# Last norm of a three-layer block: the running sum of squares moves from VectorE to GpSimd

## The reference, cut to what matters

```python
def rms_norm(x, g):
    xf = x.astype(jnp.float32)
    xf = xf * lax.rsqrt(jnp.mean(xf * xf, axis=-1, keepdims=True) + RMS_EPS)
    return xf.astype(x.dtype) * g

        x = x + hierarchical_moe(h2, ...)     # the experts' results, added to the residual
    return rms_norm(x, final_norm_g)          # over the 1024 features of each token
```

## Time and profile before

| | us |
|---|---|
| median of 3 executions | 1638.87 |
| lowest and highest of them | 1638.64, 1643.22 |
| the profiled execution, its time | 1638.95 |
| its span, first to last instruction | 1637.1 |
| around the span | 1.85 |

### The profile page before, as it was taken

How to read it: one execution, slowest core, us unless ns; L and a number is a source line. 1 busy time by engine, 2 the same in 40 slices (tenths; PEclk the granted TensorE clock), 3 DMA queues, 4 the chain that set the end, 5 groups by cost and what they waited for, 6 DMA issues and landing times.

```text
span 1637.1 us, 20086 instructions
## 1 busy us (share of the span) xinstructions
PE 1595.3 (97%) x7426; PEld 1203.3 (73%) x7426; DVE 845.6 (52%) x1456; ACT 583.0 (36%) x963; POOL 547.6 (33%) x239
## 2 busy tenths in 40 slices
PE   7999999999999999999999999999999999999997
PEld 5888768887888888887877667888877885444543
DVE  5447577125655546344668686343242644343434
ACT  4127454334332225324533342343243333112213
POOL 4441226731444444751334123455424410000000
PEclk9999999999999999999999999999999999999998
DMA  5331223521332323441222113334312349999991
GB/s 187 95 99 39 77 77 119 165 90 59 97 96 90 103 91 98 150 127 50 76 81 72 39 45 97 110 115 130 94 61 90 127 191 365 410 422 423 421 418 68
DMA packets 52787, 235.94 MB, mean 144 GB/s; under 512 B 6240, under 2 KB 7136, under 8 KB 48096
## 3 DMA queue, kind: packets, MB, share of 16 engines
q1 hardware_dynamic: 48960, 222.60, 38.8%
q0 software_dynamic: 2016, 7.34, 1.1%
q10 hardware_dynamic: 1728, 4.87, 0.9%
HBM read 230.59 MB, written 4.19 MB: 143 GB/s over the span
## 4 chain that ended last, share of the span: by engine, by line
PE 90%; DVE 6%; issue 2%; ACT 2%; DMA 0%; SPq 0%; DVEq 0%; ACTq 0%
PE G L1803 69%; PE O L1803 7%; PE S L1803 6%; PE TR L1803 4%; PE TR L1913 2%; DVE sumsq L993 1%; PE G L2370 1%; DVE sq L1053 1%; DMA w_ring<-in_stream_dram 0%; ACT hi_ring L569 0%; DVE U L1024 0%; DVE sumsq L1123 0%; DVE arena L1423 0%; DVE U L1780 0%; DVE arena L1202 0%
## 5 line engine op out<-in xcount | busy, mean ns | idle before, releaser
L534 POOL TENSOR_TENSOR lo_ring<-w_ring,hi_ring 128x1024 fp32r<-128x1024 f32 x219 | 533.9, 2439 | 788.9 <-ACT hi_ring L569 788.6
L569 ACT ACTIVATE hi_ring<-w_ring 128x1024 fp32r<-128x1024 f32 x219 | 231.3, 1059 | 588.7 <-PE G L1803 584.5
L1803 PE MATMUL G<-xa_hi,hi_ring 128*128 128x512 f32 x928 | 378.4, 408 | 9.7 <-DVE xa_lo L1115 9.6
L1803 PE MATMUL G<-xa_lo,hi_ring 128*128 128x512 f32 x928 | 364.6, 393 | 0.0
L1803 PE MATMUL G<-xa_hi,lo_ring 128*128 128x512 f32 x928 | 364.1, 392 | 0.0
L1803 PEld LDWEIGHTS G<-xa_hi,hi_ring 128*128 128x128 f32 x928 | 175.1, 189 | 50.1 <-issue 12.2
L1803 PEld LDWEIGHTS G<-xa_lo,hi_ring 128*128 128x128 f32 x928 | 175.1, 189 | 39.1 <-issue 2.6
L1803 PEld LDWEIGHTS G<-xa_hi,lo_ring 128*128 128x128 f32 x928 | 174.8, 188 | 39.4
L1803 PE MATMUL G<-yb_hi,hi_ring 128*128 128x512 f32 x388 | 154.4, 398 | 3.1 <-ACT arena L667 2.2
L1803 PE MATMUL G<-yb_hi,lo_ring 128*128 128x512 f32 x388 | 151.7, 391 | 0.0
L1803 PE MATMUL G<-yb_lo,hi_ring 128*128 128x512 f32 x388 | 151.3, 390 | 0.0
(11 more groups left out here) (350 smaller groups left out, 2503.8 us busy)
## 6 DMA issues: line engine op xcount, KB each, us to landing
w_ring<-in_stream_dram SPq DMA_DIRECT2D x219, 512.0 KB, 3.5
arena<-in_w_gu_dram SPq DMA_DIRECT2D x16, 2048.0 KB, 11.7
ex_rings<-in_w_dn_dram SPq DMA_DIRECT2D x40, 512.0 KB, 15.6
ex_low<-in_w_gu_dram SPq DMA_DIRECT2D x8, 2048.0 KB, 18.1
ex_rings<-in_w_gu_dram SPq DMA_DIRECT2D x8, 2048.0 KB, 15.7
arena<-in_w_dn_dram SPq DMA_DIRECT2D x16, 512.0 KB, 14.0
sq<-in_w_dn_dram SPq DMA_DIRECT2D x8, 512.0 KB, 17.6
X<-in_x_in_dram SPq DMA_DIRECT2D x8, 256.0 KB, 5.8
```

The lines of the kernel that those rows point to most:

```text
L534: nc.gpsimd.tensor_tensor(lo_ring[:, s, :], w_ring[:, s, :], hi_ring[:, s, :], ALU.subtract).then_inc(low, 1)
L569: nc.scalar.activation(hi_ring[:, m % RING, :], w_ring[:, m % RING, :], ACT.Copy).then_inc(high, 1)
L1803: return nc.tensor.matmul(*args, **kw)
```

## The change

GpSimd gets the running sum of the first six squares. After its last `fetch_rows` it waits until `O` and `sumsq` are free (`col_full`), then for the squares of tiles 0 and 1, and adds these two into `sumsq` in one instruction, which raises `ssq` by 2. Tiles 2 to 5 follow, each with a wait for its square and one for the addition before it. These are five 128x512 additions. In VectorE's list the last quad of the first round has no sums any more: it runs `add` 0 to 7 one after the other. The squares on ScalarE, the column products on TensorE and all later steps stay as they are.

```diff
@@ -548,6 +548,14 @@
             more_rounds = pool.value_load(overflow[0:1, 0:1])
             with pool.Fori(1, QUADS) as it:
                 fetch_rows(it)
+            base = NB["f2"][1]
+            pool.wait_ge(col_full, NB["f2"][0])
+            pool.wait_ge(xsq, base + 2)
+            nc.gpsimd.tensor_tensor(sumsq[:, :], sq[:, 0, :], sq[:, 1, :], ALU.add).then_inc(ssq, 2)
+            for f in range(2, SUMMED):
+                pool.wait_ge(xsq, base + f + 1)
+                pool.wait_ge(ssq, base - 1 + f)
+                nc.gpsimd.tensor_tensor(sumsq[:, :], sumsq[:, :], sq[:, f % 2, :], ALU.add).then_inc(ssq, 1)
             with pool.If(more_rounds > 0):
                 with pool.Fori(QUADS, ROUNDS * QUADS) as it:
                     fetch_rows(it)
@@ -1761,9 +1769,8 @@
                 quad(first, 0, before=False, primed=isinstance(rd, int))
                 with dve.Fori(1, QUADS - 1) as r:
                     quad(r + first, r)
-                quad(first + (QUADS - 1), QUADS - 1, more=False, squares=isinstance(rd, int))
-                if not isinstance(rd, int):
-                    add(first + (QUADS - 1), 4, KT)
+                quad(first + (QUADS - 1), QUADS - 1, more=False, squares=False)
+                add(first + (QUADS - 1), 4, KT)
```

## The result

| | kernel before | changed kernel |
|---|---|---|
| median, us | 1640.04 (16 executions) | 1644.68 (16 executions) |
| lowest to highest | 1637.46 to 1643.24 | 1643.44 to 1649.29 |
| ratio | | 1.0028, 95% interval 1.0019 to 1.0037 |
| profiled execution, span | 1638.95, 1637.1 | 1643.89, 1642.1 |

The change makes the kernel slower, by 0.28%, which is just under what I called the limit of a measurement. The forecast was 1641.1 (0.13% slower), in a range of 1638.9 to 1643.4. The measured time lies outside that range. The direction held; the difference, 4.64 between the medians, was twice the forecast's 2.2, and the median of the kernel before was itself no longer the 1638.87 that I had started from.

What follows compares the result with a forecast made beforehand. The prediction took the completion of sumsq, which TensorE's column products wait for, to bound the kernel. GpSimd's slower chain (+1.2) and the clock (+1.0) made +2.2, so 1641.1 us, in a range of 1638.9 to 1643.4.

Steps and rivals of the forecast that it cites:

- What bounds the kernel: Last part: the time when sumsq is complete, 1620.22, sets the end; VectorE's load matters only through that.
- four signs of being wrong: GpSimd row under 1.0, addition to X beyond 1, products waiting for tile 7's square, or clock staying full.
- GpSimd's chain, +1.2: Five dependent GpSimd additions, with waits, complete the sum at 1621.44 instead of 1620.22; ends +0.7 and +1.8 us.
- The clock, +1.0: TensorE's 24 column products, started later, run more at half clock: 4.4 instead of 3.44 us; ends 0 and +1.7.
- if the clock falls at the same time: Condition for the column products: clock falls at 1622.4 as before, so only 7.8 products fit at full clock.
- What costs nothing: GpSimd's new waits, tile 7's square, ScalarE's table load, the spread and later steps: no cost beyond shifting.
- Sum, +2.2: Whole kernel: +1.2 for GpSimd's chain and +1.0 for the clock, giving a median of 1641.1 us, 0.13% slower.
- How the numbers follow: Step from forecast to range and chances: executions differed by 4.6, so medians move by about 1; forecast itself 90%.
- 1 (GpSimd under 1.0 us): Rival: GpSimd's 128x512 additions are faster than thought, the sum comes earlier; -1.6 us, 1637.3; chance 3%.
- 2 (the engines lock each other out): Rival: VectorE's additions to X and GpSimd's additions block each other in the last part; +5.4 us, 1644.3; chance 4%.
- 3 (a late first addition): Rival: GpSimd's first addition waits 5 us or more for its code to be brought in again; 1647; chance 3%.
- Within 0.3%: Chance that the time is not told from no change: 0.91; over 1643.8 had 0.08, under 1634.0 had 0.01.

Runs made afterwards that it cites:

- e1: The changed kernel with twelve unused 128x512 matmuls on TensorE ahead of its wait for the sum; ratio 1.0008 to the kernel before.
- e3: The kernel before with three extra 128x512 additions on VectorE ahead of its last sum, nothing on GpSimd; ratio 1.0014.
- g4: The kernel before, VectorE's sums in place, with five unused 128x512 additions of two SBUF inputs on GpSimd beside them; one execution, 1648.75 us.
- e4: The kernel before with two unused 128x512 matmuls in TensorE's wait for the sum and six in its wait for the diagonal matrix; ratio 0.9999.
- h2: e4 once more, unchanged; ratio 1.0004 to the kernel before.
- h1: e4 with three more unused fp32 128x256 matmuls in TensorE's wait ahead of the experts' ranking; ratio 0.9998 to the kernel before.

## Why the prediction was off, point by point

- **What bounds the kernel: right.** The completion of `sumsq` set the end. VectorE's relief came (0.99 apart, forecast 0.95) and was worth nothing. None of the four signs of being wrong appeared.
- **GpSimd's chain, +1.2: it was +1.7**, inside the ends given (+0.7 to +1.8). The pieces, from the change's first profile: start 0.18 after the square (0.08 forecast), 1.26 to 1.30 an addition (1.25), 0.13 before each dependent one (0.08), 0.80 for the square in between (0.75). Every one was on the low side, because I took the latency of the quickest row and the fixed cost of a memset. In sum 7.82 instead of 7.32.
- **The clock, +1.0: it was +0.8 on the mean**, and +1.85 in the first pair of profiles. The latter is beyond the far end of +1.7. Mechanism and sign were right (e1 and e3). The changed kernel's products took 4.53 on the mean, against 4.4 forecast, and that is in part luck: "if the clock falls at the same time" didn't hold, the fall came 0.4 later than the 8.28 of the first profile and the products began 0.5 later than forecast, which nearly cancel. What I missed besides is that the base moves as well, the 3.44 of the profile that I read being a favourable case of a mean of 3.73.
- **What costs nothing: right.** The square of tile 7 ended at 1624.29, ahead of its products; nothing waited for GpSimd's list otherwise.
- **Sum, +2.2: the last part measured +2.5.** The measured median is 3.6 over the forecast. Of this, 0.3 is the last part, 1.2 is the base (1640.04 instead of 1638.87), and 2.1 is what the change's executions took beyond both. So the step that failed is the one behind the sum, in "How the numbers follow": "Executions of one kernel differed by 4.6, so the median of a few can move by about 1". The medians of the kernel before, each of 16 to 35 executions, were 1640.04, 1641.31, 1642.42, 1641.49 and 1640.68, so 1.2 to 3.6 over the 1638.87 of three executions; single ones went from 1636.1 to 1645.9. With it fails a term that the forecast put at nothing: a difference upstream of the last part, 1.63 in the first pair of profiles and 2.6 on the mean of five. Each of the two was more than the 1.0 allowed for both. The 2.1 is spread and what may be steady upstream, and its cause stays open.
- **Rivals.** 1 (GpSimd under 1.0 us) fell with the first row. 2 (the engines lock each other out) didn't happen in the change, and g4 shows why: the lock is real, but it holds for two SBUF inputs only, and the additions to X have one from PSUM. 3 (a late first addition) fell: the first started 0.18 after its square and took 1.29, like the others.
- **The chances.** "Within 0.3%" had 0.91, and the ratio is 1.0028 with an interval to 1.0037; it came true narrowly, and only because the base rose too: in us, 1644.68 lies over the 1643.8 that had 0.08.

## What to carry to other kernels

Moving work off an engine helps only if that engine's load was what the critical wait stood for; here the wait was for one result, and handing its making to an engine that needs 1.43 a step for it instead of 1.20 (an addition to X included) delayed it. A chain of dependent steps is to be costed with its own waits and with the buffers that tie its producer to it: these were 1.2 of the 7.8 us. And where an effect of 0.1% is to be forecast in us, the level needs many executions of the kernel before; three, two of them 0.23 us apart, set it 1.2 us too low or more. A fixed point in both traces then tells how much of a difference was there before the change could act.

## What the runs showed of the hardware

- GpSimd combines two fp32 operands from SBUF in 0.18 us plus 2.2 ns a column (additions of 256 and 512 columns 0.74 and 1.29, subtractions of 1024 columns 2.40), and needs 0.13 more where it waits for its own last result.
- VectorE and GpSimd instructions that both read two operands from SBUF hold each other up (0.68 to 1.20, 1.29 to 1.54), and one with an operand from PSUM doesn't take part. The Trainium skill (SBUF — State Buffer, section "SBUF: two separate sides") states this lock; these rows agree.
- Twelve wide matmuls with no use in a wait of 2.9 us kept the clock at 2.4 GHz through 24 thin products behind them, 2.84 instead of 4.1 to 5.3 (e1, one profile). Two in the kernel before's shorter wait did the same in three profiles (2.85 to 2.93, against 3.33 to 4.17 without them); six in the next wait held it in one profile and not in two (e4, h2, h1).
- The same 1600 us of work ended up to 9 us apart from one execution to another, with 13.6 to 30.8 us at half clock; the two go together only loosely (correlation 0.70 over 18 profiles; e1 and the change's first profile both have 23.9 and lie 2.8 apart), so the clock isn't all of that spread.
